# Splitting value tiles 1 to 3 of an attention projection into upper and lower parts, and reordering the last scores around state products (one Trainium2 core)

## The chip, the cores and the metric

One core of a Trainium2 chip (trn2) runs the whole program; the other cores are idle. The metric is the device time of one execution in microseconds. Three executions of the kernel before took 428.85 to 428.94 us, median 428.89 us. TensorE (PE in the profile), VectorE (DVE), ScalarE (ACT), GpSimd (POOL) and the DMA queues of SyncE (SP) each run their own instruction stream and meet at semaphores.

## The reference, cut to what matters

The program is one layer of a hybrid encoder on 512 tokens of width 1024, in float32. What the change touches is the attention group and, through queues and order, its two neighbours:

```python
z = x @ w_in                                  # x: 512 x 1024
u_pool, q, k, v, u_ssm = split(z)             # widths 256, 384, 384, 384, 384
y_pool = pool_mixer(u_pool, ...)              # trailing means over 2, 4, 8, 16 tokens, then a small product
s  = q k^T / 8 + bias, masked                 # 6 heads of 64, chunks of 64 tokens, 8 earlier chunks
y_attn = softmax(s) @ v
y_ssm = s5_mixer(u_ssm, ...)                  # state space, GELU, gated linear unit (GLU)
heads = concat(rms(y_pool), rms(y_attn), rms(y_ssm))
h = layer_norm(alpha * x + heads @ w_out)
# then a routed mixture of 16 experts, a gated per-layer embedding (PLE), and a second layer norm
```

## The kernel before, in words

Tokens are four tiles of 128. The input stands transposed in `xT` (region E, 8 blocks of 128 input channels by 512 tokens). A float32 product on TensorE is issued as two MATMUL records for each `matmul` call. The kernel already has a second way to make such a product: both operands are split into an upper part (ScalarE copies the tensor into a tile of type fp32r, which rounds it) and a lower part (VectorE subtracts the upper from the original, again as fp32r), and three fp32r products, upper by upper, lower by upper and upper by lower, are summed in PSUM with one MATMUL record each. The state input, queries, the first keys, the GLU (`glu`, L1139), the output projection and the PLE gate are made so.

Nothing is planned by a program: each engine's order is written out by hand, and semaphores join them. Around the change, from about 85 to 137 us of the span, the orders are these.

TensorE: `scores(1)`, value tile 0 (`v_tile`, L998, 8 calls of 128x384), the state products (L1117 to L1124: three groups of eight, two calls of 64 columns for each, into banks 7, 0, 6), `scores(2)` (L1126), value tile 1, the transposes of the softmax of heads 0 and 1 (`turn_probs`, L1040, three units of transposes for each head), value tile 2, heads 2 and 3, value tile 3, heads 4 and 5, then the GLU (L1171), the pooling product (L1179), `weigh_values` (L1061) and the output projection. `turn_probs` reuses three PSUM banks, so that each unit waits for the copy out of the unit three before it; heads 0, 1, 4, 5 are copied out by ScalarE (`pt_copy`), heads 2 and 3 by VectorE (`pt_move`, L1652).

VectorE: from `s_ready` (end of the state rotation) on it does `normalise` 0 and 1 (the softmax's division, L1581), `add_bias` 2 and 3 (scores out of PSUM, L1555), `row_max` 2 and 3 (L1573), `normalise` 2 and 3, the lower part of the GLU weights (L1644), `add_bias` 4 and 5, `row_max` 4 and 5, then three additions of the skip term to the state output (L1651, both tensors in SBUF), `normalise(4)`, `pt_move` 2 and 3, `normalise(5)` and the three lower parts of the GELU output (L1664).

ScalarE: copies of queries and keys out of PSUM, `pool_copy(1)`, the upper part of the GLU weights (L746), `v_copy(0)`, the exponents of heads 2 and 3 (`exps`, L723), three copies `y_copy` of the state output (L771), `v_copy(1)`, `pt_copy` 0 and 1, the exponents of heads 4 and 5, three GELUs (L789), their upper parts, `v_copy` 2 and 3, and so on.

The state output goes to DRAM and back in another layout on SyncE's queue: three transfers out, each after its `y_copy` (L370), and when all three have landed three back (L374), which L1651 waits for. Behind them on the same queue stand the loads of `w_out` (4096 KB), `x` (2048 KB) and the PLE gate weights.

GpSimd: after `pool_copy(1)` it makes the trailing means (`add_shift`, L559 to L574: L568 is the fourth step of ten) and signals `pool_ready`; later it adds squares (L580).

Of the kernel before, what the change touches and what calls it, by code (L numbers as in the profile page):

```python
# [19 lines left out]
ALU = mybir.AluOpType  # L20
ACT = mybir.ActivationFunctionType
AX = mybir.AxisListType

P = 128
D = 1024
T = 512
# [7 lines left out]
CH = 8  # L34
# [45 lines left out]
V_BANKS = (6, 7, 2, 5)  # L80
PM_BANKS = (7, 0)
# [32 lines left out]
def trunk(nc, io, out):  # L114
    with ExitStack() as ctx:
# [109 lines left out]
        def over(name, cols, at):  # L225
            return nc.alloc_sbuf_tensor_at(name, [P, cols], F32R, offset=at)
# [26 lines left out]

        pp_hi = over("ple_proj_upper", 2 * D, G0 + 4 * 2048)
# [7 lines left out]
        def dram(name, shape, dt=F32):  # L262
# [47 lines left out]
            "u_out u_back m0_in s_ready s_moved y_evac y_out y_back yin_ready gelu_done glu_lo_set glu_sig ssm_done "  # L310
# [19 lines left out]
        def _(sp):  # L330
            def load(dst, src, signal):
                sp.dma_start(dst, src).then_inc(S[signal], 16)
# [40 lines left out]
            for m in range(3):  # L373
                load(yT[:, m, :].rearrange("p (j c) -> p j c", j=CH), y_d.rearrange("j f c -> f j c")[m * P:(m + 1) * P], "y_back")  # L374

            sp.wait_ge(S["rot_ready"], 3)
            load(w_o, io["w_out"].rearrange("(k p) n -> p k n", p=P), "wo_in")

            sp.wait_ge(S["s_read"], HEADS)
            load(xh, io["x"].rearrange("(t p) d -> p t d", p=P), "xh_in")  # L380

            w_pg_v = io["w_ple_gate"].rearrange("(p k) n -> p k n", k=KD)
            load(w_pg[:, 0, 0:6], w_pg_v[:, 0:6, 0:512], "wpg0_in")
            sp.wait_ge(S["pool_ready"], 1)
# [97 lines left out]
        def _(gp):  # L482
# [84 lines left out]
            add_shift(b2, a, 2, 64, slice(0, 1))  # L567
            link(g.tensor_copy(a[64:P, 0:1], b2[64:P, 0:1]))  # L568
# [81 lines left out]
        def _(ac):  # L650
# [92 lines left out]
            qk_copy(5)  # L743
            pool_copy(1)
            ac.wait_ge(S["wglu_in"], 16)
# [34 lines left out]
            for m in range(3):  # L780
                y_copy(m)
# [3 lines left out]
            exps(4)  # L785
            exps(5)
# [35 lines left out]
            ac.wait_ge(S["wo_in"], 16)  # L822
# [123 lines left out]
        def _(pe):  # L946
# [55 lines left out]

            def scores(pair):
# [108 lines left out]
            v_tile(0, V_BANKS[0])  # L1112

# [11 lines left out]
            pe.wait_ge(S["s_read"], 4)  # L1125
            scores(2)  # L1126

            pe.wait_ge(S["y_evac"], 1)
            v_tile(1, V_BANKS[1])
            turn_probs(0)  # L1130
            turn_probs(1)
            v_tile(2, V_BANKS[2])
            turn_probs(2)
            turn_probs(3)
            v_tile(3, V_BANKS[3])
# [49 lines left out]
            pe.wait_ge(S["wo_in"], 16)  # L1185
# [254 lines left out]
        def _(dv):  # L1440
# [199 lines left out]
            row_max(3)  # L1640
            normalise(2)
# [3 lines left out]
            add_bias(4)  # L1645
            add_bias(5)
            row_max(4)
            row_max(5)
            dv.wait_ge(S["y_back"], 48)
# [8 lines left out]
            normalise(4)  # L1658
# [389 lines left out]
```

## Time and profile before

| | us |
|---|---|
| median of 3 executions | 428.89 |
| the profiled execution's own time | 429.05 |
| its span (first to last instruction) | 427.30 |
| TensorE busy in the span | 413.3 (97%) |
| VectorE busy | 255.4 (60%) |
| ScalarE busy | 129.6 (30%) |
| GpSimd busy | 93.6 (22%) |
| granted TensorE clock, mean | 0.993 of full |

Busy time counts every record; a MATMUL record lasts longer than the distance to the next one, since matmuls are pipelined. So for TensorE the distance between starts is what a product costs. In a timeline row the first number is the start in us from the span's start, the second the time to the end of the merged group, then engine, line, operation, output<-input, shapes, count, and in brackets the idle time before it and what ended it.

### The profile page before, as it was taken

The page shows a single profiled execution, that of the slowest core. Times are in us where ns is not written, and L with a number is a line of the kernel's source. Part 1 is how long each engine was busy: PE and PEld are TensorE (multiplying, and loading weights), DVE is VectorE, ACT ScalarE, POOL GpSimd, SP SyncE. Part 2 cuts the span into 40 slices and gives each one's busy share as a digit, 9 for nine tenths or more (in the row PEclk, how much of TensorE's full clock was granted, in tenths as well). Part 3 has the DMA queues.
Part 4 walks back from the last instruction along what each step waited for, and adds up shares of the span by engine and source line. Part 5 has one row for each costly group of instructions (what it writes and reads, how often), then busy time and mean ns, then how long its engine had stood idle before and what let it go on. Part 6 is the DMA issues. An engine that isn't in the chain of part 4 may idle for free.

```text
span 427.3 us, 5594 instructions
## 1 busy us (share of the span) xinstructions
PE 413.3 (97%) x2167; PEld 238.1 (56%) x2167; DVE 255.4 (60%) x464; ACT 129.6 (30%) x235; POOL 93.6 (22%) x132
## 2 busy tenths in 40 slices
PE   8899999999999999999999999999999999999992
PEld 5677655469667555676577887333333433333271
DVE  2999985986873999998867524211101112224987
ACT  4721336025497890200621011011110111111243
POOL 2830269275000800000000742010111111000000
PEclk9999999999999999999999999999999999999997
DMA  7994103251997891111490428999999999977313
GB/s 264 431 397 129 49 2 66 68 130 51 276 411 295 285 392 63 49 49 51 158 384 8 191 43 325 425 410 413 418 417 418 421 411 411 423 289 247 152 45 153
DMA packets 33626, 102.76 MB, mean 240 GB/s; under 512 B 14882, under 2 KB 16082, under 8 KB 26816
## 3 DMA queue, kind: packets, MB, share of 16 engines
q1 hardware_dynamic: 26032, 92.79, 56.1%
q0 software_dynamic: 4016, 7.97, 5.6%
q10 hardware_dynamic: 3552, 1.65, 1.4%
q8 instruction: 17, 0.28, 0.3%
q14 instruction: 9, 0.07, 0.1%
HBM read 93.29 MB, written 15.24 MB: 254 GB/s over the span
## 4 chain that ended last, share of the span: by engine, by line
PE 67%; issue 23%; DVE 4%; DMA 3%; POOL 1%; ACT 1%; DVEq 0%; POOLq 0%; ACTq 0%
PE bank L1307 20%; PE bank L1317 10%; PE bank L952 7%; PE bank L1000 5%; PE bank L1302 3%; PE bank L967 3%; PE bank L992 3%; PE bank L1009 2%; PE bank L988 2%; PE bank L1067 2%; PE bank L1057 2%; POOL slot_scratch L595 1%; PE bank L995 1%; PE bank L1123 1%; PE bank L1122 1%
## 5 line engine op out<-in xcount | busy, mean ns | idle before, releaser
L1307 PE MATMUL bank<-region_a,region_g 128*64 128x512 f32 (+1 forms) x224 | 77.8, 594 | 0.0
L1317 PE MATMUL bank<-region_a,region_c 128*64 128x512 f32 (+1 forms) x160 | 43.7, 596 | 0.0
L1885 DVE TENSOR_TENSOR region_c<-region_c,bank 128x256 f32<-128x256 f32 x12 | 5.1, 421 | 64.6 <-ACT region_c L907 64.6
L1307 PE MATMUL bank<-region_h,region_g 128*64 128x512 f32 (+1 forms) x96 | 42.4, 594 | 0.0
L1307 PE MATMUL bank<-region_b,region_g 128*64 128x512 f32 (+1 forms) x96 | 42.4, 594 | 0.0
L1307 PE MATMUL bank<-region_c,region_g 128*32 128x512 f32 (+1 forms) x96 | 42.4, 594 | 0.0
L1878 DVE COPY region_g<-bank 128x512 f32<-128x512 f32 x24 | 15.5, 687 | 40.4 <-PE bank L1302 40.4
L1307 PEld LDWEIGHTS bank<-region_a,region_g 128*64 128x64 f32 (+1 forms) x224 | 22.2, 123 | 25.1 <-issue 24.4
L1151 PE MATMUL bank<-region_b,region_e 128*128 128x512 f32 x68 | 32.9, 607 | 0.0
L907 ACT ACTIVATE region_c<-bank 128x256 f32<-128x256 f32 x12 | 4.6, 384 | 83.9 <-PE bank L1307 83.9
L952 PE MATMUL bank<-region_e,region_a 128*128 128x512 f32 x64 | 28.0, 595 | 0.0
L595 POOL DMA_INDIRECT slot_scratch<-region_h,slot_i x8 | 8.2, 1027 | 88.3 <-issue 88.3
L1235 PE MATMUL bank<-ple_gate_upper,hidden_upper 128*128 128x512 f32 x64 | 25.7, 402 | 0.0
L1237 PE MATMUL bank<-ple_gate_upper,hidden_lower 128*128 128x512 f32 x64 | 25.0, 390 | 0.0
L1236 PE MATMUL bank<-ple_gate_lower,hidden_upper 128*128 128x512 f32 x64 | 24.9, 390 | 0.0
L1317 PEld LDWEIGHTS bank<-region_a,region_c 128*64 128x64 f32 (+1 forms) x160 | 12.0, 123 | 22.1 <-issue 22.0
L1317 PE MATMUL bank<-region_c 128*32 128x512 f32 (+1 forms) x48 | 21.9, 596 | 0.0
L1317 PE MATMUL bank<-region_b,region_c 128*64 128x512 f32 (+1 forms) x48 | 21.7, 595 | 0.0
L1000 PE MATMUL bank<-region_a,region_e 128*128 128x384 f32 x64 | 21.5, 489 | 0.0
L952 PEld LDWEIGHTS bank<-region_e,region_a 128*128 128x128 f32 x64 | 12.0, 190 | 14.5 <-issue 14.4
L608 POOL DMA_INDIRECT expert_scratch<-region_g,region_h x5 | 5.0, 1002 | 65.2 <-ACT region_g L890 65.2
L1722 DVE SCALAR_TENSOR_TENSOR region_f<-bank,rms_r,region_f 128x512 f32<-128x512 f32 x24 | 18.0, 750 | 2.0 <-PE bank L1151 1.3
(364 smaller groups left out, 881.9 us busy)
## 6 DMA issues: line engine op xcount, KB each, us to landing
region_a<-in_w_exp_down SPq DMA_DIRECT2D x10, 1024.0 KB, 14.4
region_a<-in_w_exp_gate SPq DMA_DIRECT2D x7, 1024.0 KB, 8.4
region_a<-in_w_exp_up SPq DMA_DIRECT2D x7, 1024.0 KB, 12.1
region_b<-in_w_out SPq DMA_DIRECT2D x1, 4096.0 KB, 14.7
expert_scratch<-zero_scratch SPq DMA_DIRECT2D x8, 512.0 KB, 9.5
region_c<-in_w_ple_gate SPq DMA_DIRECT2D x2, 1536.0 KB, 23.1
region_b<-in_w_exp_gate SPq DMA_DIRECT2D x3, 1024.0 KB, 10.3
region_b<-in_w_exp_up SPq DMA_DIRECT2D x3, 1024.0 KB, 12.3
```

The lines of the kernel that those rows point to most:

```text
L952: last = mm(bank[bank_i][:], w[:, k, m * P:(m + 1) * P], xT[:, k, :], start=(k == 0), stop=(k == KD - 1))
L967: last = mm(bank[m][:], w[:, k * SSM_W + m * P:k * SSM_W + (m + 1) * P], x[:, k * T:(k + 1) * T], start=False, stop=(stop and k == 5))
L992: mm(dst, w_hi[:, k * width + m * P:k * width + (m + 1) * P], x[:, k * T:(k + 1) * T], start=False, stop=False)
L1000: last = mm(bank[bank_i][:, 0:ATT_W], xT[:, k, t * P:(t + 1) * P], w_v[:, k, :], start=(k == 0), stop=(k == KD - 1))
L1151: last = mm(bank[WO_AT[half][group]][:], hdT[:, k, t * P:(t + 1) * P], w_o[:, k, half * 512:half * 512 + 512], start=(i == 0), stop=(i == ...
L1235: mm(bank[PG_AT[k % 2]][:], h_hi[t][:, x], pg_hi[:, w], start=(c == 0), stop=False)
L1236: mm(bank[PG_AT[k % 2]][:], h_hi[t][:, x], pg_lo[:, w], start=False, stop=False)
L1237: last = mm(bank[PG_AT[k % 2]][:], h_lo[t][:, x], pg_hi[:, w], start=False, stop=(c == KD - 1))
L1307: return mm(out_[at:at + width].rearrange("p (u n) -> p u n", u=2), x[:, k, at:at + width], w[:, k], start=(k == 0), stop=(k == KD - 1), t ...
L1317: return mm(bank[banks[half]][at:at + width, :], act_e[:, r, 2, k * P + at:k * P + at + width], w[:, k, half * 512:half * 512 + 512], star ...
L1722: last = stt(xh[:, t, cols], bank[WO_AT[half_][group]][:], rms_r[:, group, t:t + 1], xh[:, t, cols], ALU.mult, ALU.add)
L1878: v.tensor_copy(hgT[:, t % 2, 4 * u:4 * u + 4, :], bank[B_TOK[u]][:].rearrange("p (k s) -> p k s", k=4)).then_inc(S["hgT_evac"], 1)
```

## The change

Value tiles 1 to 3 are made by a new function `v_split`: 24 fp32r products in place of 8 float32 calls. The upper parts of the value weights and of `xT` are made by ScalarE in two pieces each, between the copies it does from 80 us on. The lower part of the input is made by GpSimd in the middle of the pooling, in place over `xT`, after value tile 0 has read it; GpSimd then waits until five heads are normalised before it goes on with the pooling. The lower part of the value weights is made by VectorE. `scores(2)` goes ahead of the state products. On VectorE `add_bias` and `row_max` of heads 4 and 5 and `normalise(4)` move ahead; on ScalarE the exponents of heads 4 and 5 go between the three `y_copy`. The last quarter of `w_out`, the first half of the PLE gate weights and `x` are loaded only after value tile 3, since the new tiles lie where they land.

The list of semaphores (`y_back` goes, `gp_lo_set` comes) is left out of the diff.

```diff
@@ -78,6 +78,7 @@
 KERN_BANKS = (1, 2)
 X_BANKS = ((3, 7), (0, 6))
 V_BANKS = (6, 7, 2, 5)
+XV_PARTS, WV_PARTS = ((0, 5), (5, KD)), ((0, 6), (6, KD))
 PM_BANKS = (7, 0)
 Y_BANKS = (7, 0, 6)
 PV_BANKS = (5, 6, 3)
@@ -251,6 +252,13 @@
         kw_lo = over("key_weights_lower", 6 * ATT_W, A0 + 4 * (O_K + 2 * ATT_W))
         uw_lo = over("state_weights_lower", 6 * SSM_W, A0 + 4 * 2 * SSM_W)
 
+        F0 = R0 + 4 * 4096
+        XV_AT, WV_AT = (F0 + 4 * 1536, B0 + 4 * 6656), (C0 + 4 * 768, A0 + 4 * 13440)
+        xv_hi = [over(f"value_input_upper{i}", (hi - lo) * T, XV_AT[i]) for i, (lo, hi) in enumerate(XV_PARTS)]
+        wv_hi = [over(f"value_weights_upper{i}", (hi - lo) * ATT_W, WV_AT[i]) for i, (lo, hi) in enumerate(WV_PARTS)]
+        xv_lo = over("value_input_lower", KD * T, R0)
+        wv_lo = over("value_weights_lower", KD * ATT_W, A0 + 4 * O_V)
+
         pp_hi = over("ple_proj_upper", 2 * D, G0 + 4 * 2048)
         pp_lo = over("ple_proj_lower", 2 * D, H0)
         p_hi = over("ple_input_upper", 2 * T, G0 + 4 * 1024)
@@ -371,16 +379,18 @@
                              y_ch[:, 8 * m:8 * m + 8, :].rearrange("p g c -> p (g c)")).then_inc(S["y_out"], 16)
             sp.wait_ge(S["y_out"], 48)
             for m in range(3):
-                load(yT[:, m, :].rearrange("p (j c) -> p j c", j=CH), y_d.rearrange("j f c -> f j c")[m * P:(m + 1) * P], "y_back")
+                load(yT[:, m, :].rearrange("p (j c) -> p j c", j=CH), y_d.rearrange("j f c -> f j c")[m * P:(m + 1) * P], "y_out")
 
             sp.wait_ge(S["rot_ready"], 3)
-            load(w_o, io["w_out"].rearrange("(k p) n -> p k n", p=P), "wo_in")
-
+            w_o_v = io["w_out"].rearrange("(k p) n -> p k n", p=P)
+            load(w_o[:, 0:6], w_o_v[:, 0:6], "wo_in")
+            sp.wait_ge(S["pe_v"], NT)
+            load(w_o[:, 6:KD], w_o_v[:, 6:KD], "wo_in")
+
+            w_pg_v = io["w_ple_gate"].rearrange("(p k) n -> p k n", k=KD)
+            load(w_pg[:, 0, 0:6], w_pg_v[:, 0:6, 0:512], "wpg0_in")
             sp.wait_ge(S["s_read"], HEADS)
             load(xh, io["x"].rearrange("(t p) d -> p t d", p=P), "xh_in")
-
-            w_pg_v = io["w_ple_gate"].rearrange("(p k) n -> p k n", k=KD)
-            load(w_pg[:, 0, 0:6], w_pg_v[:, 0:6, 0:512], "wpg0_in")
             sp.wait_ge(S["pool_ready"], 1)
             load(w_pg[:, 1, 2:8], w_pg_v[:, 2:8, 512:D], "wpg_in")
             sp.wait_ge(S["pe_pm"], 2)
@@ -565,6 +575,13 @@
             add_shift(a, plT, 1, 0, both)
             add_shift(b2, a, 2, 0, second)
             add_shift(b2, a, 2, 64, slice(0, 1))
+            gp.wait_ge(S["xw_hi_set"], 12)
+            gp.wait_ge(S["pe_v"], 1)
+            for (lo, hi), upper in zip(XV_PARTS, xv_hi):
+                at = slice(lo * T, hi * T)
+                g.tensor_tensor(xv_lo[:, at], RE[:, at], upper[:], ALU.subtract).then_inc(S["gp_lo_set"], 1)
+            gp.wait_ge(S["gp_lo_set"], 2)
+            gp.wait_ge(S["p_norm"], HEADS - 1)
             link(g.tensor_copy(a[64:P, 0:1], b2[64:P, 0:1]))
             add_shift(a, b2, 4, 0, second)
             link(g.tensor_copy(b2[64:P, 1:2], a[64:P, 1:2]))
@@ -741,7 +758,18 @@
             exps(1)
             qk_copy(4)
             qk_copy(5)
+
+            def value_weights_upper(i):
+                at = slice(O_V + WV_PARTS[i][0] * ATT_W, O_V + WV_PARTS[i][1] * ATT_W)
+                a.activation(wv_hi[i][:], RA[:, at], ACT.Copy).then_inc(S["xw_hi_set"], 1)
+
+            ac.wait_ge(S["wv_in"], 32)
+            value_weights_upper(0)
             pool_copy(1)
+            value_weights_upper(1)
+            ac.wait_ge(S["s_ready"], 1)
+            for (lo, hi), upper in zip(XV_PARTS, xv_hi):
+                a.activation(upper[:], RE[:, lo * T:hi * T], ACT.Copy).then_inc(S["xw_hi_set"], 1)
             ac.wait_ge(S["wglu_in"], 16)
             a.activation(wg_hi[:], w_glu.rearrange("p k n -> p (k n)"), ACT.Copy).then_inc(S["gelu_done"], 1)
 
@@ -777,13 +805,14 @@
             exps(2)
             exps(3)
             ac.wait_ge(S["s_moved"], 64)
-            for m in range(3):
-                y_copy(m)
+            y_copy(0)
+            exps(4)
+            y_copy(1)
+            exps(5)
+            y_copy(2)
             v_copy(1)
             pt_copy(0)
             pt_copy(1)
-            exps(4)
-            exps(5)
             for m in range(3):
                 ac.wait_ge(S["yin_ready"], m + 1)
                 a.activation(geluT[:, m, :].rearrange("p (c j) -> p c j", j=CH),
@@ -819,7 +848,7 @@
             ac.wait_ge(S["pool_mixed"], 2)
             for k in WO_SPLIT:
                 a.activation(hd_hi[k][:], hdT[:, k, P:T], ACT.Copy).then_inc(S["wo_hi_set"], 1)
-            ac.wait_ge(S["wo_in"], 16)
+            ac.wait_ge(S["wo_in"], 32)
             for k in (0, 1, 5, 6, 7):
                 a.activation(wo_hi[k][:], w_o[:, k, :], ACT.Copy).then_inc(S["wo_hi_set"], 1)
 
@@ -1000,6 +1029,21 @@
                     last = mm(bank[bank_i][:, 0:ATT_W], xT[:, k, t * P:(t + 1) * P], w_v[:, k, :], start=(k == 0), stop=(k == KD - 1))
                 last.then_inc(S["pe_v"], 1)
 
+            def v_split(t, bank_i):
+
+                def upper(parts, homes, width, k, at, w):
+                    i = 0 if k < parts[0][1] else 1
+                    first = (k - parts[i][0]) * width + at
+                    return homes[i][:, first:first + w]
+
+                for term, (signal, count) in enumerate((("xw_hi_set", 12), ("gp_lo_set", 2), ("xw_lo_set", 10))):
+                    pe.wait_ge(S[signal], count)
+                    for k in range(KD):
+                        x = xv_lo[:, k * T + t * P:k * T + t * P + P] if term == 1 else upper(XV_PARTS, xv_hi, T, k, t * P, P)
+                        w = wv_lo[:, k * ATT_W:(k + 1) * ATT_W] if term == 2 else upper(WV_PARTS, wv_hi, ATT_W, k, 0, ATT_W)
+                        last = mm(bank[bank_i][:, 0:ATT_W], x, w, start=(term == 0 and k == 0), stop=(term == 2 and k == KD - 1))
+                last.then_inc(S["pe_v"], 1)
+
             def scores(pair):
 
                 def part(odd, tile):
@@ -1110,6 +1154,8 @@
             scores(1)
             pe.wait_ge(S["wv_in"], 32)
             v_tile(0, V_BANKS[0])
+            pe.wait_ge(S["s_read"], 4)
+            scores(2)
 
             pe.wait_ge(S["s_moved"], 64)
             pe.wait_ge(S["m0_in"], 16 * CH * 2)
@@ -1122,17 +1168,15 @@
                     mm(dst, m0[:, g].rearrange("p l h -> p (l h)"), uch[:, g, :], start=True, stop=False)
                     last = mm(dst, cp[:, g, 1:CH + 1, :].rearrange("p l h -> p (l h)"), s_in[:, g, :], start=False, stop=True)
                 last.then_inc(S["pe_y"], 1)
-            pe.wait_ge(S["s_read"], 4)
-            scores(2)
 
             pe.wait_ge(S["y_evac"], 1)
-            v_tile(1, V_BANKS[1])
+            v_split(1, V_BANKS[1])
             turn_probs(0)
             turn_probs(1)
-            v_tile(2, V_BANKS[2])
+            v_split(2, V_BANKS[2])
             turn_probs(2)
             turn_probs(3)
-            v_tile(3, V_BANKS[3])
+            v_split(3, V_BANKS[3])
             turn_probs(4)
             turn_probs(5)
 
@@ -1182,7 +1226,7 @@
             for pair in range(3):
                 weigh_values(pair)
 
-            pe.wait_ge(S["wo_in"], 16)
+            pe.wait_ge(S["wo_in"], 32)
             pe.wait_ge(S["pool_mixed"], 2)
             pe.wait_ge(S["glu_sig"], 3)
             pe.wait_ge(S["sq_added"], 3)
@@ -1638,15 +1682,21 @@
             add_bias(3)
             row_max(2)
             row_max(3)
+            add_bias(4)
+            add_bias(5)
+            row_max(4)
+            row_max(5)
+            dv.wait_ge(S["xw_hi_set"], 10)
+            dv.wait_ge(S["pe_v"], 1)
+            for (lo, hi), upper in zip(WV_PARTS, wv_hi):
+                tt(wv_lo[:, lo * ATT_W:hi * ATT_W], RA[:, O_V + lo * ATT_W:O_V + hi * ATT_W], upper[:],
+                   ALU.subtract).then_inc(S["xw_lo_set"], 1)
             normalise(2)
             normalise(3)
             dv.wait_ge(S["gelu_done"], 1)
             tt(wg_lo[:], w_glu.rearrange("p k n -> p (k n)"), wg_hi[:], ALU.subtract).then_inc(S["glu_lo_set"], 1)
-            add_bias(4)
-            add_bias(5)
-            row_max(4)
-            row_max(5)
-            dv.wait_ge(S["y_back"], 48)
+            normalise(4)
+            dv.wait_ge(S["y_out"], 96)
             for m in range(3):
                 stt(yT[:, m, :], uT[:, m, :], vec[:, V_D + m:V_D + m + 1], yT[:, m, :], ALU.mult, ALU.add).then_inc(S["yin_ready"], 1)
             def pt_move(h):
@@ -1655,7 +1705,6 @@
                     dv.wait_ge(S["pe_pt"], k + 1)
                     v.tensor_copy(probT[h // 2][:, h % 2, o:o + w], bank[PT_BANKS[k % 3]][:, 0:w]).then_inc(S["pt_moved"], 1)
 
-            normalise(4)
             pt_move(2)
             pt_move(3)
             normalise(5)
```

## Rows read from the trace of the kernel before

**Rows 1.** The page's chain that ended last: share of the span by engine

```profile
PE 67%; issue 23%; DVE 4%; DMA 3%; POOL 1%; ACT 1%; DVEq 0%; POOLq 0%; ACTq 0%
```

**Rows 2.** Timeline of PE, 78 to 95 us: start, us, engine, line, operation, shapes, count

```profile
94.44 0.33 PE L1122 MATMUL bank<-region_h 128*128 128x64 f32 x2
```

**Rows 3.** Timeline of PE, 95 to 160 us, same columns

```profile
105.20 2.43 PE L1009 MATMUL bank<-region_g 64*128 64x256 f32 x16
107.56 5.43 PE L1000 MATMUL bank<-region_a,region_e 128*128 128x384 f32 x16
...
115.32 5.33 PE L1000 MATMUL bank<-region_a,region_e 128*128 128x384 f32 x16
120.48 1.25 PE L1057 MATMUL bank<-ident,region_a 128*128 128x128 f32 x10
121.96 1.38 PE L1057 MATMUL bank<-ident,region_a 128*128 128x128 f32 x10 [0.22 <-DVE region_a L1656]
...
131.07 0.39 PE L1144 MATMUL bank<-gelu_lower,glu_upper 128*128 128x512 f32 x1
...
136.76 0.40 PE L1145 MATMUL bank<-gelu_upper,glu_lower 128*128 128x512 f32 x1
```

**Rows 4.** Timeline of VectorE (DVE), 66 to 162 us: scores, row maxima, softmax, moves

```profile
89.29 0.62 DVE L1569 SCALAR_TENSOR_TENSOR region_a<-bank,region_f 128x128 f32<-128x128 f32 x2 [1.29 <-PE bank L1009]
...
92.98 3.23 DVE L1578 TENSOR_REDUCE att_mx<-region_a 128x1 f32<-128x128 f32 x8
...
98.05 4.58 DVE L1587 TENSOR_SCALAR region_a<-region_a,att_sm 128x128 f32<-128x128 f32 x4
...
102.75 1.27 DVE L1587 TENSOR_SCALAR region_a<-region_a,att_sm 128x128 f32<-128x128 f32 x4
103.94 1.35 DVE L1644 TENSOR_TENSOR glu_lower<-region_a,glu_upper 128x1152 fp32r<-128x1152 f32 x1
...
114.51 2.07 DVE L1651 SCALAR_TENSOR_TENSOR region_h<-region_h,vec 128x512 f32<-128x512 f32 x3
...
121.12 3.15 DVE L1656 COPY region_a<-bank 128x512 f32<-128x512 f32 x6 [0.78 <-PE bank L1057]
```

**Rows 5.** Timeline of ScalarE (ACT), 66 to 162 us

```profile
93.66 1.17 ACT L746 ACTIVATE glu_upper<-region_a 128x1152 fp32r<-128x1152 f32 x1 [6.13 <-DMA region_a<-in_w_glu]
...
95.10 0.39 ACT L729 ACTIVATE region_a<-region_a,att_mx 128x128 f32<-128x128 f32 x1
...
100.32 0.58 ACT L773 ACTIVATE region_b<-bank 128x512 f32<-128x512 f32 x1
...
105.31 0.60 ACT L773 ACTIVATE region_b<-bank 128x512 f32<-128x512 f32 x1 [2.98 <-PE bank L1123]
```

**Rows 6.** Timeline of GpSimd (POOL), 66 to 162 us: the pooling

```profile
92.80 0.61 POOL L568 COPY region_c<-region_c 64x512 f32<-64x512 f32 x1
...
95.77 1.25 POOL L562 TENSOR_TENSOR region_c<-region_c 64x504 f32<-64x504 f32 x1
97.10 2.36 POOL L573 TENSOR_TENSOR region_c<-region_c 128x1024 f32<-128x1024 f32 x1
99.53 2.48 POOL L574 TENSOR_TENSOR region_c<-region_c,region_g 128x1024 f32<-128x1024 f32 x1
```

**Rows 7.** Tile y_scratch, 108.95 to 109.3 us: the last transfer back, issue and landing

```profile
L332 SPq DMA_DIRECT2D region_h<-y_scratch x1: 880/880/880, 109.0 to 109.0; - x1
...
DMA to landing us min/median/max: 4.6/4.6/4.6
```

**Rows 8.** Timeline of GpSimd (POOL), 66 to 162 us: later sums

```profile
140.26 3.72 POOL L580 TENSOR_TENSOR region_g<-region_g,region_a 128x512 f32<-128x512 f32 x2 [0.51 <-ACT region_a L769]
```

**Rows 9.** Timeline of VectorE (DVE), 66 to 162 us: later differences

```profile
140.67 2.18 DVE L1672 TENSOR_TENSOR ple_gate_lower<-region_c,ple_gate_upper 128x1024 fp32r<-128x1024 f32 x1
...
144.57 1.22 DVE L1672 TENSOR_TENSOR ple_gate_lower<-region_c,ple_gate_upper 128x1024 fp32r<-128x1024 f32 x1
```

**Rows 10.** The page's DMA issues: KB each, us from issue to landing

```profile
region_b<-in_w_out SPq DMA_DIRECT2D x1, 4096.0 KB, 14.7
```

More of the change, by code:

```diff
@@ L309, in trunk @@
             "kern_in kern_done rot_ready xrot_done "
-            "u_out u_back m0_in s_ready s_moved y_evac y_out y_back yin_ready gelu_done glu_lo_set glu_sig ssm_done "
+            "u_out u_back m0_in s_ready s_moved y_evac y_out gp_lo_set yin_ready gelu_done glu_lo_set glu_sig ssm_done "
             "pool_ready pool_mixed pe_u pe_qk pe_pool pe_v pe_bxT pe_kern pe_x pe_s pe_pt pe_pv pe_pm pe_y "
```

## The prediction, made before the change was run

> **What bounds the kernel now.** I read the page's busy shares and its chain first: TensorE is busy 97% of the span and holds most of the chain [rows 1] (the part called issue begins behind 149 us and runs past a stretch in which TensorE's records stand back to back, so I take it as TensorE time too). Then I read TensorE's timeline through the changed stretch. From the first state product at 94.44 us [rows 2] to the GLU near 131 us it has one idle gap of 0.22 us, before the transposes of head 3 at 121.96 us, which waited for VectorE's copy L1656 [rows 3]. So a product made shorter here is worth its full length, as long as every new helper is early enough, and anything that makes VectorE late at L1656 is paid in full. That gap is the place to watch: value tiles 1 and 2 lie ahead of it, only tile 3 behind it.
>
> **The value tiles.** Value tile 2 starts at 115.32 us and the next transposes at 120.48 us: 5.16 us for 16 records of 384 columns, 0.322 us each [rows 3]. The price of an fp32r product is in the GLU: from its record at 131.07 us to that at 136.76 us are 25 starts, 5.69 us, 0.228 us for 512 columns [rows 3]. No row has 384 columns of fp32r. From below: all of it scales with the columns, 0.171 us. From above: it doesn't shrink at all, 0.228 us. A moving tile is read column by column in either type, so I take a value near the lower end, with a little of the 0.228 us fixed: 0.174 us. 24 of them are 4.18 us, 0.98 us less for each tile (bounds: 1.06 less, 0.31 more). Three tiles: 2.9 us less if nothing waits.
> On this the Trainium skill (TensorE: Matmul & The Clock Gate, Back-to-back issue gap) gives columns over 2.4 GHz plus 2.5 ns, an estimate of 162 ns for 384 columns; the GLU's rows are 12 ns above that formula. By it each tile would gain 1.3 us.
>
> **scores(2) ahead of the products.** The two only change places: the scores take 2.36 us (105.20 to 107.56), the products 10.76 us [rows 2, 3]. The scores wait for `add_bias(3)`, which ended with the start of the row maxima at 92.98 us [rows 4], before 94.44 us: no wait. The products now run from 96.8 to 107.56 us, and value tile 1 starts at 107.56 us, as before. Their three groups end 2.4 us later each.
>
> **The helpers of the split.** ScalarE copies 7168 columns more, at 1.17 us for 1152 about 7.3 us; it stood idle 6.1 us before 93.66 us and about as long between the earlier key and pool copies [rows 5], so it is done by about 92.5 us: nothing. If that cover were gone, 7.3 us would fall on `exps`.
> GpSimd waits for value tile 0 (94.7 us). 1024 columns of a two-tensor operation take 2.36 us [rows 6]; 4096 columns 9.1 to 9.4 us, so it is done at 104.0 us. TensorE wants this part at 107.56 + 1.4 = 109.0 us: nothing. VectorE's operations in that time are scores from PSUM and row maxima. Eight row maxima took 3.23 us, 0.4 us each, with GpSimd busy beside them from 92.80 us on [rows 4, 6]: no room for a wait on a sum of 1 us or more, so these don't disturb each other. Scores of two heads took 3.69 us (89.29 to 92.98 us).
> VectorE: `add_bias` 4 and 5 from 96.9 to 100.6, `row_max` to 103.8 us. The lower weights, 2304 and 768 columns at 1.35 us for 1152 [rows 4], are 3.5 us; they begin when GpSimd's second piece ends, 104.1 us, and end at 107.5 us, wanted at 110.3 us: nothing. Then `normalise` 2 and 3 (1.4 us each with the reciprocal), the GLU's lower weights 1.3 us, `normalise(4)`: 113.0 us. Here GpSimd goes on.
>
> **The two engines meet.** The rest of the pooling ran from 92.80 to 102.01 us; its third sum starts 2.97 us after L568 and lasts 1.25 us, then come two of 1024 columns [rows 6]. Begun at 113.1 us, that third sum runs from 116.0 to 117.3 us and the rest to 122.3 us.
> The state output: `y_copy(0)` at 100.5 us, exponents of head 4 from 102.3 us (its row maxima end there) for 2.61 us (two heads from 95.10 to 100.32 us [rows 5]), `y_copy(1)`, exponents of head 5 to 108.1 us, `y_copy(2)` to 108.7 us instead of 105.9 us. The last transfer back was issued at 109.0 us and landed 4.6 us later, 113.6 us [rows 7]; now 116.4 us.
> At 116.4 us VectorE wants L1651, three operations on two SBUF tensors (2.07 us together [rows 4]), while GpSimd is in that third sum. What happens then is in two places. L1587, 1.27 us when alone, took 4.58 us from 98.05 us, until both large pooling sums were over [rows 4, 6]. And L1672 (two SBUF tensors) took 2.18 us beside GpSimd's L580 and 1.22 us where it came first, while the two L580 took 3.72 us, not 2 times 1.27 us or less [rows 8, 9]: the engines take turns, each operation waits for the other engine's present one. So: first L1651 at 117.3 us, 0.66 us; a large sum, 2.28 us; second L1651; the second large sum; third L1651, ending at 117.3 + 3 x 0.66 + 2 x 2.25 = 123.8 us. Bounds: 118.5 us with no turns at all, 123.8 us with all; I take the upper, since L1651 is nearest to L1672 in its operands.
> The Trainium skill (SBUF — State Buffer, the section on two separate sides) says why: VectorE and GpSimd share one port pair under an exclusive lock, and a VectorE operation with two SBUF inputs takes it too. The trace agrees for L1672; for a SCALAR_TENSOR_TENSOR like L1651 no row shows it.
>
> **What is late next.** Behind L1651 on VectorE stand the copies L1656 of head 2. They began at 121.12 us before; TensorE would now be ready for them at 119.2 us, but gets them from 123.8 us: 2.7 us later than before, all that tiles 1 and 2 gained lost. Head 3's transposes start 2.7 us late, tile 3 gives 1.0 us back, and the GLU starts 1.7 us late. Its lower GELU parts (the last L1651 123.8, a GELU, upper copies, `normalise(5)`, L1664) are ready near 130.3 us, the GLU wants them at 132.4 us: hidden. From there all is TensorE again and shifts as a whole.
>
> **The queues.** On SyncE's queue 3072 KB of w_out leave as before; 1024 KB, then 1536 KB of PLE gate weights and `x` now wait for tile 3 (about 130 us). 4096 KB landed in 14.7 us [rows 10], so the first 2560 KB need at most 9.2 us, 139.5 us, about when VectorE is through with the GLU's gates; `x` is wanted 20 us later. I cost it at nothing; without that cover 1 us on VectorE. `pool_ready`, 22 us later than before, holds back a PLE load that already waits in the queue, and a TensorE wait that comes after the GLU: nothing.
>
> **The sum.** 429.05 + 2.7 - 1.0 = 430.75 us against the profiled execution; that stood 0.16 us above the median, so 430.6 us.
>
> **The rivals.** A measurement of this kernel can tell about 0.2% (0.86 us) from no change.
> (a) VectorE's L1651 takes no turns with GpSimd. It ends at 118.5 us, L1656 follows TensorE, and all three tiles count: 428.9 - 2.9 = 426.0 us, faster. For it: the row maxima were not held up, and L1651 is another kind of operation than L1672. Against: it reads two tensors in SBUF, as L1672 does. It decides from the point at which L1651 ends before 119.2 us. Chance 0.27.
> (b) They take turns, but the transfer lands before the third sum begins, or VectorE reaches 113.0 us half a microsecond later. Only 0.4 us lie between 116.0 and 116.4 us. Then the first L1651 goes ahead of that sum and one turn of 2.3 us falls away: L1651 ends at 121.5 us, 0.4 us of delay against 1.0 us gained, 428.3 us. Chance 0.2.
> (c) fp32r with 384 columns costs as with 512: tile 3 is 0.3 us longer instead of 1.0 us shorter, 431.9 us with the turns. Against: float32 records do shrink with their columns. Chance 0.03.
> (d) The change doesn't do what it says: the tiles wait for their lower parts. VectorE is 2.8 us early, GpSimd 5 us; it would take an operation nearly half as slow again. Included in 0.02 for anything else, such as a late load.
>
> **How the numbers follow.** My case has chance 0.48; with (c) and half of the rest slower has 0.52. (b) is within 0.2%: 0.19. Faster is (a) and a little of (b): 0.29. The likeliest case's own range is 429.9 to 431.2 us (a turn's start 0.7 us either way); for 8 in 10 it reaches down to (a), 425.8 us, and up to 431.4 us.
>
> **What would show it.** Right: L1651 takes about 7 us for three in place of 2.07; TensorE waits 4 to 5 us for L1656 before head 3; tiles 1 to 3 last 4.2 us each. The GLU starts near 132.5 us. Wrong: three L1651 in about 2.1 us beside busy GpSimd; no TensorE wait for L1656; a GLU at 127.8 us; or a wait at the second or third term of value tile 1.

## The result, and the profile after

The changed kernel took 432.37 us (median of five executions: 431.33, 431.35, 432.37, 432.45, 432.46) against 428.89 us for the kernel before: 3.5 us slower between the medians; the ratio over all executions, two of which were 1 us faster than the other three, is 1.0069 with a 95% interval of 1.0058 to 1.0080. The forecast was 430.6 us, range 425.8 to 431.4: the right side, half the size, and the range missed by 1 us. The profiled execution has 432.37 us and a span of 430.6 us, 3.3 us more than the 427.3 us of before. Its TensorE is busy 96% of the span and its mean granted clock over the span is 0.987 of full, 0.993 before. The other two executions near 432.4 us show 0.987 too, the two at 431.3 us 0.990 and 0.991.

TensorE's timeline through the changed stretch (start, us, then as before; L1044 is `v_split`, L1101 `turn_probs`, L1188 the GLU):

```profile
107.51 1.66 PE L1044 MATMUL bank<-value_weights_upper,value_input_upper 128*128 128x384 f32 x8
109.01 1.55 PE L1044 MATMUL bank<-value_weights_upper,value_input_lower 128*128 128x384 f32 x8
110.40 1.55 PE L1044 MATMUL bank<-value_weights_lower,value_input_upper 128*128 128x384 f32 x8
...
118.45 1.25 PE L1101 MATMUL bank<-ident,region_a 128*128 128x128 f32 x10
123.80 2.37 PE L1101 MATMUL bank<-ident,region_a 128*128 128x128 f32 x10 [4.10 <-DVE region_a L1706]
125.82 2.91 PE L1044 MATMUL bank<-value_weights_upper,value_input_upper 128*128 128x384 f32 x8
128.53 1.92 PE L1044 MATMUL bank<-value_weights_upper,value_input_lower 128*128 128x384 f32 x8
130.28 1.55 PE L1044 MATMUL bank<-value_weights_lower,value_input_upper 128*128 128x384 f32 x8
131.67 2.66 PE L1101 MATMUL bank<-ident,region_a 128*128 128x128 f32 x20
...
134.40 0.40 PE L1188 MATMUL bank<-gelu_lower,glu_upper 128*128 128x512 f32 x1
```

Value tile 1 starts at 107.51 us, where before it started at 107.56 [rows 3]. Eight fp32r products of 384 columns take 1.39 us (109.01 to 110.40), 0.174 us each, and tile 1 lasts to 111.78 us, 4.3 us in place of 5.2. Then the transposes of head 3 wait 4.10 us for VectorE's copy. And behind this wait everything on TensorE is slow: the transposes of head 3 take from 123.80 to 125.82 us, 2.02 us where ten others cost some 1.2, and tile 3's three groups of eight take 2.7, 1.75 and 1.39 us. The GLU's second product comes at 134.40 us instead of 131.07 [rows 3]: 3.33 us, the whole difference of the spans.

Busy time of each engine in stretches behind the wait (the first number behind the last engine, POOL, is the granted TensorE clock):

```profile
core 0: us, PE busy (x) PEld busy (x) DVE busy (x) ACT busy (x) POOL busy (x), PEclk, DMA share, GB/s
118.00:124.00 6.00, 1.90 (x15) 1.66 (x14) 6.00 (x4) 2.70 (x3) 4.43 (x2) 0.87 0.89 358
124.00:126.00 2.00, 2.00 (x11) 2.00 (x11) 1.50 (x4) 1.97 (x5) 0.00 (x0) 0.50 0.06 23
126.00:128.00 2.00, 2.00 (x8) 2.00 (x8) 1.97 (x7) 0.25 (x1) 0.00 (x0) 0.50 0.00 0
128.00:130.00 2.00, 2.00 (x10) 2.00 (x9) 2.00 (x4) 0.00 (x0) 0.00 (x0) 0.67 0.00 0
130.00:132.00 2.00, 2.00 (x15) 1.97 (x13) 0.01 (x1) 0.13 (x1) 0.00 (x0) 1.00 0.00 0
```

The granted clock is 0.50, the lower level of 1.2 GHz, from 122.5 us, when TensorE had stood idle since 119.7 us, to past 129 us, and full again from 129.5 us on. The Trainium skill (TensorE: Matmul & The Clock Gate, part on the clock gate) says that TensorE drops to half its clock after idling and comes back only after work. The trace agrees, with 0.50 in these rows. It is a price that the prediction didn't have.

VectorE's and GpSimd's timelines (L1692 the lower value weights, L1631 `normalise`, L1701 the skip additions, L1706 the copies of heads 2 and 3; L582 the lower input, L572 and L590, L591 sums of the pooling):

```profile
103.71 3.42 DVE L1692 TENSOR_TENSOR value_weights_lower<-region_a,value_weights_upper 128x2304 fp32r<-128x2304 f32 x2
...
111.32 1.27 DVE L1631 TENSOR_SCALAR region_a<-region_a,att_sm 128x128 f32<-128x128 f32 x4
116.11 6.94 DVE L1701 SCALAR_TENSOR_TENSOR region_h<-region_h,vec 128x512 f32<-128x512 f32 x3 [3.51 <-DMA region_h<-y_scratch]
122.97 1.61 DVE L1706 COPY region_a<-bank 128x512 f32<-128x512 f32 x3
```

```profile
94.65 9.05 POOL L582 TENSOR_TENSOR value_input_lower<-region_e,value_input_upper 128x2560 fp32r<-128x2560 f32 x2 [2.18 <-PE bank L1029]
112.73 0.61 POOL L585 COPY region_c<-region_c 64x512 f32<-64x512 f32 x1 [9.03 <-DVE region_a L1631]
...
115.70 1.26 POOL L572 TENSOR_TENSOR region_c<-region_c 64x504 f32<-64x504 f32 x1
117.05 2.70 POOL L590 TENSOR_TENSOR region_c<-region_c 128x1024 f32<-128x1024 f32 x1
119.83 2.68 POOL L591 TENSOR_TENSOR region_c<-region_c,region_g 128x1024 f32<-128x1024 f32 x1
```

The three skip additions took 6.94 us, not 2.07 [rows 4]. They came at 116.11 us, while the third sum of the pooling ran (115.70 to 116.96 us); each of the two large sums, 2.37 us when nothing of VectorE's takes turns with it (e8), shows 2.7 us here, since each began by waiting for the end of an addition. The engines took turns, as L1672 and L580 did before [rows 8, 9].

### The profile page after: what moved, and what is told of

The parts are those of the page before. It is cut to its first block, busy times and chain, and to the rows that moved or that the text cites. A ratio compares the mean times of both kernels' runs of the same rounds, so it can differ in the third digit from the quotient of the medians.

```text
span 430.6 us, 5655 instructions
## 1 busy us (share of the span) xinstructions
PE 413.5 (96%) x2191; PEld 244.4 (57%) x2191; DVE 260.4 (60%) x466; ACT 136.0 (32%) x239; POOL 102.5 (24%) x134
## 4 chain that ended last, share of the span: by engine, by line
PE 61%; issue 23%; DVE 7%; DMA 4%; ACT 3%; POOL 1%; SPq 0%; DVEq 0%; POOLq 0%; ACTq 0%
PE bank L1351 20%; PE bank L1361 10%; PE bank L981 6%; PE bank L1346 3%; PE bank L996 3%; PE bank L1021 3%; PE bank L1053 2%; DVE region_h L1701 2%; PE bank L1017 2%; PE bank L1111 2%; POOL slot_scratch L612 1%; PE bank L1044 1%; PE bank L1024 1%; PE bank L1029 1%; ACT region_a L746 1%
## 5 line engine op out<-in xcount | busy, mean ns | idle before, releaser
L1351 PEld LDWEIGHTS bank<-region_h,region_g 128*64 128x64 f32 (+1 forms) x96 | 11.4, 123 | 12.5 <-issue 12.2
```

Of the source, the lines that this page charges most:

```text
L1351: return mm(out_[at:at + width].rearrange("p (u n) -> p u n", u=2), x[:, k, at:at + width], w[:, k], start=(k == 0), stop=(k == KD - 1), t ...
```

## The experiments

All are made from the changed kernel, each timed in five rounds beside the kernel before on the same chip (its medians there are 428.96 to 429.10 us; the changed kernel's time is that of the result above). The two questions: is it GpSimd's turns that make VectorE late and so cost TensorE its wait, and is the rest of the loss the clock?

### e1: the pooling goes on only after the skip additions

```diff
             gp.wait_ge(S["p_norm"], HEADS - 1)
+            gp.wait_ge(S["yin_ready"], 3)
```

> GpSimd goes on with the pooling only when VectorE's three skip additions (L1651 of before) are done. Theory (the two engines take turns, and the delay of the copies of head 2 is what TensorE pays): the three additions take 2.1 us in place of 6.9, TensorE doesn't wait before head 3, its granted clock stays at full, and the three tiles take 4.2 us each. But the pooling now meets normalise(5) and the lower GELU parts on VectorE, which end near 130 us, so TensorE waits about 2 us before the GLU: 428.3 us. Rival (the additions are slow for another reason, such as the w_out transfer beside them): still 6.9 us, time 432.4 us. Rival (fp32r products of these operands are slow by themselves): tile 3 still 5.8 us and the time at least 429.5 us.

Measured: 428.25 us (427.81 to 430.27), ratio 0.9992 (0.9981 to 1.0004). VectorE's rows, and what TensorE waited for:

```profile
115.88 2.08 DVE L1702 SCALAR_TENSOR_TENSOR region_h<-region_h,vec 128x512 f32<-128x512 f32 x3 [3.38 <-DMA region_h<-y_scratch]
118.97 3.14 DVE L1707 COPY region_a<-bank 128x512 f32<-128x512 f32 x6 [1.02 <-PE bank L1102]
...
122.24 5.64 DVE L1632 TENSOR_SCALAR region_a<-region_a,att_sm 128x128 f32<-128x128 f32 x4
```

```profile
PE bank L1102 <- DVE region_a L1632: 1.5, 1, 1.5
...
PE bank L1188 <- DVE gelu_lower L1714: 0.5, 1, 0.5
```

The additions take 2.08 us, with the same w_out transfer beside them, so it was GpSimd. TensorE waits 0.22 us before head 3, as in the kernel before. But the pooling now takes its turns with `normalise(5)`, 5.64 us in place of 1.28, and TensorE waits 1.5 us before head 5 and 0.5 us before the GLU: some 2 us, as expected, but most of it two steps earlier. The wait was moved some 7 us down the line. It wasn't harmless there in every execution: eight of the twelve took 427.8 to 428.5 us with a mean clock of 0.993 to 0.996, the profiled one among them (1.00 behind the wait), and four took 429.5 to 430.3 us with 0.990 to 0.991. These four fit a fall of the clock that no profile shows.

### e2: TensorE kept busy during the wait

```diff
             turn_probs(2)
+            for _ in range(19):
+                mm(bank[4][:], xv_lo[:, 0:P], xv_lo[:, 0:T], start=True, stop=True)
             turn_probs(3)
```

> As after, but TensorE makes 19 fp32r products of 512 columns into an unused bank between the transposes of heads 2 and 3, 4.3 us in place of the 4.1 us wait; nothing reads them. Theory (tile 3 was slow since the granted clock fell to 1.2 GHz after the idle 4.1 us): the granted clock stays at full, tile 3 takes 4.2 us in place of 5.8, time about 430.6 us, which is what was forecast. Rival (tile 3 is slow because of its operands or of transfers beside it): tile 3 still 5.8 us, time 432.5 us or more.

Measured: 430.14 us (429.96 to 430.64), ratio 1.0027 (1.0016 to 1.0038). TensorE's timeline and two stretches:

```profile
119.51 4.61 PE L1179 MATMUL bank<-value_input_lower 128*128 128x512 f32 x19
123.95 1.33 PE L1101 MATMUL bank<-ident,region_a 128*128 128x128 f32 x10
125.04 1.64 PE L1044 MATMUL bank<-value_weights_upper,value_input_upper 128*128 128x384 f32 x8
...
129.29 2.66 PE L1101 MATMUL bank<-ident,region_a 128*128 128x128 f32 x20
```

```profile
120.00:130.00 10.00, 10.00 (x59) 9.01 (x59) 9.38 (x16) 4.85 (x8) 2.61 (x1) 1.00 0.31 123
130.00:140.00 10.00, 9.88 (x48) 7.29 (x48) 3.44 (x6) 7.66 (x14) 0.55 (x1) 1.00 0.91 352
```

TensorE reaches head 3 at 123.95 us, 0.15 us later than in the changed kernel, and yet the program is 2.2 us faster. The clock is 1.00 throughout, tile 3 takes 4.25 us (125.04 to 129.29) in place of 5.85, head 3 takes 1.1 us in place of 2.0. Operands, transfers and order are those of the changed kernel; only the idle stretch is gone. So the fall of the clock cost 2.2 us in the median execution, and what is left, 1.1 us over the kernel before, is the lateness of head 3 (2.0 us) less tile 3's gain. Also the two groups of the changed kernel's times, 431.3 and 432.4 us, are one group here (429.96 to 430.64 us, mean clock 0.993 to 0.995). With the mean clocks of the two groups, 0.990 to 0.991 and 0.987, this fits a lower clock that lasted for different times from execution to execution; no profile of the faster group shows it.

### e7: half of the wait busy

```diff
             turn_probs(2)
+            for _ in range(9):
+                mm(bank[4][:], xv_lo[:, 0:P], xv_lo[:, 0:T], start=True, stop=True)
             turn_probs(3)
```

> As e2, but 9 products, 2.05 us, so that some 2 us of TensorE's wait for VectorE stay idle. Theory (it is the length of the idle stretch that brought the clock down; the 1.8 us wait of e3 left it at full): full clock, tile 3 in 4.2 us, 430.2 us as e2. Rival (a wait there brings the clock down whatever its length): tile 3 longer than 4.5 us and 431.3 us or more.

Measured: 430.26 us (430.16 to 430.48 in four executions, 431.72 in the fifth), ratio 1.004 (1.0027 to 1.0053). What TensorE waited for, and its clock:

```profile
PE bank L1101 <- DVE region_a L1708: 2.1, 1, 2.1
```

```profile
120.00:130.00 10.00, 7.91 (x50) 7.12 (x49) 9.40 (x16) 4.74 (x8) 2.63 (x1) 1.00 0.32 131
```

Idle for 2.1 us, TensorE keeps its clock (1.00), and the time is e2's. The fifth execution, 1.5 us slower, isn't the profiled one, but its mean clock over the span is 0.991, against 0.993 to 0.994 in the other four: most likely the clock fell in it. So the length of the wait counts (four executions of five come out as the theory has it, while at 4.1 us the mean clock is lower in all five), but it doesn't decide alone: 2.1 us cost only themselves as a rule, and once some 1.5 us more.

### e3: GpSimd isn't held at all

```diff
-            gp.wait_ge(S["p_norm"], HEADS - 1)
```

> GpSimd doesn't wait for the fifth normalised head: the pooling goes on at 103.8 us. Theory (turns): it now takes turns with the lower value weights and normalise 2 to 4 on VectorE; each of them waits for a pooling operation, normalise(4) ends near 120 us instead of 112.7, the skip additions then run undisturbed but late, to about 123 us, and the time stays within 1 us of 432.4 us. Rival (only the skip additions suffer): the pooling is over before 116 us, the additions take 2.1 us, 426.0 us.

Measured: 427.69 us (427.56 to 427.89), ratio 0.9967 (0.9954 to 0.9980): between the two expectations, nearer to the rival's, and faster than the kernel before. VectorE, GpSimd, and TensorE's wait:

```profile
103.88 3.41 DVE L1691 TENSOR_TENSOR value_weights_lower<-region_a,value_weights_upper 128x2304 fp32r<-128x2304 f32 x2
...
112.10 3.52 DVE L1696 TENSOR_TENSOR glu_lower<-region_a,glu_upper 128x1152 fp32r<-128x1152 f32 x1
...
118.87 2.07 DVE L1700 SCALAR_TENSOR_TENSOR region_h<-region_h,vec 128x512 f32<-128x512 f32 x3
```

```profile
103.92 3.85 POOL L584 COPY region_c<-region_c 64x512 f32<-64x512 f32 x1
...
114.48 3.40 POOL L590 TENSOR_TENSOR region_c<-region_c,region_g 128x1024 f32<-128x1024 f32 x1
```

```profile
PE bank L1100 <- DVE region_a L1705: 1.8, 1, 1.8
```

VectorE and GpSimd did meet, but the turns were not strict: GpSimd's copy at 103.92 us, 0.61 us when alone, waited through both parts of the lower value weights (3.85 us), `normalise(4)` ended at 118.9 us, not 120, and the skip additions followed at once. They ran undisturbed in 2.07 us. TensorE waited 1.8 us at full clock, and all five executions lie within 0.3 us. With the large sums where the change has them, the hold for `normalise` is therefore what hurts: it shields operations that nobody waits for and puts the pooling's largest sums beside the three that TensorE is waiting for.

### e8: the copies ahead of the skip additions

```diff
             normalise(4)
-            dv.wait_ge(S["y_out"], 96)
-            for m in range(3):
-                stt(yT[:, m, :], ...)
...
             pt_move(2)
             pt_move(3)
+            dv.wait_ge(S["y_out"], 96)
+            for m in range(3):
+                stt(yT[:, m, :], ...)
             normalise(5)
```

> As after, hold and all, but VectorE makes the copies of heads 2 and 3 ahead of the three skip additions. Theory (what cost the time is that these copies stood behind additions which waited for GpSimd's turns): no TensorE wait over 0.3 us before head 3, full clock; the additions come at about 122 us, when the pooling is over, and take 2.1 us; the lower GELU parts come at about 128.7 us against a GLU that could start at 127.8: 427.0 us. Rival (the additions' lateness itself costs what it did, through the GELU): 430 us or more.

Measured: 430.12 us median of 12 executions, in two groups (428.3 to 428.9 and 430.0 to 430.4), ratio 1.0016 (1.0005 to 1.0027). A miss in the time, which is the rival's (430 us or more). TensorE's waits and its clock:

```profile
PE bank L1101 <- ACT region_a L784: 2.7, 1, 2.7
...
PE bank L1101 <- DVE region_a L1703: 0.2, 1, 0.2
```

```profile
120.00:130.00 10.00, 7.34 (x50) 6.98 (x51) 7.46 (x16) 6.97 (x12) 1.85 (x1) 0.98 0.68 243
130.00:140.00 10.00, 10.00 (x39) 7.41 (x39) 3.30 (x6) 6.26 (x10) 0.42 (x1) 0.85 1.03 400
```

The part about head 3 held: 0.2 us. But the additions came at 122.1 us and the GELUs behind them, and on ScalarE's queue the copies `pt_copy(4)` stand behind the GELUs: TensorE waited 2.7 us for ScalarE before head 5, which I had not followed. It is the way of the rival, lateness through the GELU, with another wait at its end. In the profiled execution the clock fell again (0.85 in the next 10 us). The two groups of times fit executions with and without that fall: the eight slower ones have a mean clock of 0.989 to 0.991, the profiled one among them, the four faster ones 0.993 to 0.994.

### e5 and e6: each half of the change alone

e5 keeps the new order and makes tiles 1 to 3 as in the kernel before; e6 keeps the tiles in parts and puts `scores(2)`, heads 4 and 5 and `normalise(4)` where they were. Neither holds GpSimd.

```diff
-            v_split(1, V_BANKS[1])
+            v_tile(1, V_BANKS[1])
...
-            add_bias(4)
-            add_bias(5)
-            row_max(4)
-            row_max(5)
             dv.wait_ge(S["xw_hi_set"], 10)
```

(the first two lines are e5's, for each tile, with the upper and lower parts taken out; the rest is e6's, which puts the four lines behind the GLU's lower weights again and the exponents behind `pt_copy(1)`)

> The order of after (scores(2) ahead of the state products, heads 4 and 5 ahead on VectorE and ScalarE, the later loads), but value tiles 1 to 3 as float32 products and no upper or lower parts; the pooling isn't held and runs in one piece as before. Theory (the order alone only changes places): the skip additions come at 116 us instead of 114.5, take 2.1 us and are over before the copies of head 2 at 121.1 us, time 428.9 us, no change. Rival (the later round trip of the state output costs by itself): TensorE waits 1 us or more before the GLU, 430 us or more.

Measured: 429.21 us (428.89 to 429.51), ratio 1.0006 (0.9998 to 1.0015): no difference. TensorE's only wait in the stretch is the old one of 0.2 us.

> The other half alone: tiles 1 to 3 in parts, but scores(2), the exponents, the row maxima of heads 4 and 5 and normalise(4) in the order of before; the pooling isn't held. Theory (the gain of the tiles is 2.9 us and only a late VectorE takes it away): GpSimd's lower input part ends about 104 us, the pooling then runs to about 116 us and delays the skip additions by 1 to 2 turns, to about 118 us; the exponents of heads 4 and 5 stand before the GELU as before, so the lower GELU parts come about 128.4 us where the GLU could start at 127.8: 426.7 us. Rival (the reordering is needed, since the lower parts are late without it): a TensorE wait at value tile 1 and 428.5 us or more.

Measured: 434.49 us (434.20 to 434.87), ratio 1.013 (1.0116 to 1.0145). VectorE, TensorE's wait, and a stretch with the granted clock:

```profile
96.75 9.96 DVE L1686 TENSOR_TENSOR value_weights_lower<-region_a,value_weights_upper 128x2304 fp32r<-128x2304 f32 x2
...
111.51 3.51 DVE L1691 TENSOR_TENSOR glu_lower<-region_a,glu_upper 128x1152 fp32r<-128x1152 f32 x1
114.94 0.61 DVE L1611 SCALAR_TENSOR_TENSOR region_a<-bank,region_f 128x128 f32<-128x128 f32 x2
```

```profile
PE bank L1100 <- DVE region_a L1611: 6.1, 1, 6.1
```

```profile
118.00:124.00 6.00, 5.24 (x21) 5.24 (x22) 5.83 (x13) 3.69 (x11) 0.00 (x0) 0.50 0.41 162
```

A clear miss. The lower value weights, 3.4 us of work, are asked for at 96.75 us beside GpSimd's lower input, and take 9.96 us in turns; after them `normalise` and the GLU's lower weights take turns with the pooling, and `add_bias` of heads 4 and 5 comes at 114.94 us instead of 107.67 in the kernel before. TensorE needs their banks for the first transposes and waits 6.1 us, and behind this wait its clock is 0.50 too (118 to 124 us). The sum fits: 6.1 us less the 2.9 us of the tiles is 3.2 us, and the other 2.3 us of the 5.5 us lost is about what the clock cost in the changed kernel. Against e3, which has the parts, no hold and the new order, the old order costs 6.8 us. So the reordering is needed for the parts: it fills the time of GpSimd's lower input with work on PSUM and row maxima, which show no turns (eight row maxima take 3.2 us beside GpSimd's lower input, as before). In itself it neither costs nor gives (e5).

### e4, e9, e10: the two large sums wait for the lower GELU parts

```diff
             gp.wait_ge(S["rc_in"], 16)
+            gp.wait_ge(S["glu_lo_set"], 4)
             link(g.tensor_tensor(a, a, rcnt, ALU.mult))
```

> GpSimd makes the small pooling steps as in after, but its two sums of 1024 columns wait until VectorE has made the lower GELU parts. Theory: only the third pooling step stands before the skip additions, which end near 119 us instead of 123; no TensorE wait before head 3 to speak of, full clock, GLU near 127.8 us, the pooling ready near 130.5 us before TensorE wants it at 134 us: 426.0 us, the full gain of the three tiles. Rival (something else on VectorE or the lower GELU parts binds, and the tiles' gain isn't to be had): 428.5 us or more.

Measured: 426.12 us (425.70 to 426.27), ratio 0.9929 (0.9916 to 0.9942). VectorE and GpSimd:

```profile
116.26 2.60 DVE L1702 SCALAR_TENSOR_TENSOR region_h<-region_h,vec 128x512 f32<-128x512 f32 x3 [3.65 <-DMA region_h<-y_scratch]
119.13 3.15 DVE L1707 COPY region_a<-bank 128x512 f32<-128x512 f32 x6 [0.27 <-PE bank L1102]
...
123.59 1.89 DVE L1714 TENSOR_TENSOR gelu_lower<-region_h,gelu_upper 128x512 fp32r<-128x512 f32 x3
```

```profile
115.72 1.27 POOL L572 TENSOR_TENSOR region_c<-region_c 64x504 f32<-64x504 f32 x1
125.65 2.36 POOL L591 TENSOR_TENSOR region_c<-region_c 128x1024 f32<-128x1024 f32 x1 [8.66 <-DVE gelu_lower L1714]
128.09 2.41 POOL L592 TENSOR_TENSOR region_c<-region_c,region_g 128x1024 f32<-128x1024 f32 x1
```

One turn is left (2.60 us for the three additions), TensorE waits the old 0.2 us, its clock stays full, and the pooling is done at 130.5 us, before TensorE asks for it at 134.03 us. The GLU's second product comes at 128.09 us, 3.0 us earlier than in the kernel before. The tiles in parts are worth what their rows say.

> As e4 (the two sums of 1024 columns wait for the lower GELU parts), and the wait for the fifth normalised head is taken away, so that the small pooling steps start at 103.8 us beside the lower value weights. Theory: the small steps take a few turns on VectorE before 112 us, where it is some 3 us ahead of its next work, and none is left beside the skip additions, which take 2.1 us in place of 2.6; TensorE doesn't need them earlier: 426.1 us, the same as e4. Rival (the hold is worth something, since it keeps the lower weights or normalise(2) in time): a TensorE wait at value tile 1 or head 2 and 427 us or more.

Measured: 426.28 us (426.12 to 426.36), ratio 0.9931 (0.9917 to 0.9944): the same. The additions take 2.08 us, and `normalise(4)` ends 2 us later, where nobody waits.

> The same kernel as e4 once more, beside e9 on the same chip: 426.1 us, 0.7% under the kernel before. If e4's gain was luck of one chip, it is closer to 429.

Measured: 426.33 us (425.79 to 426.54), ratio 0.9929 (0.9915 to 0.9942). e4 holds: 2.8 us under the kernel before on the same chip, and 6 us under the changed one, with one line more than the latter.

## Why the prediction was right in kind and wrong in size

**The value tiles: right.** 0.174 us for a product of 384 columns was the value taken, 0.174 us is what 109.01 to 110.40 us gives; e4 shows the 2.9 us of three tiles as time. The Trainium skill's formula (TensorE: Matmul & The Clock Gate, Back-to-back issue gap), by which the prediction gave an estimate of 162 ns, is 12 ns low here, as it was for the GLU's rows.

**Order and helpers: right.** Tile 1 started within 0.1 us of the forecast and waited for none of its parts: GpSimd's was done at 103.7 us (104.0 forecast), VectorE's at 107.1 (107.5), `normalise(4)` at 112.6 (113.0). e5 shows the order costs nothing. That transfers behind tile 3 cost nothing is borne out by e4, where they too leave only after tile 3 and the whole 2.9 us arrives.

**The turns: right, slightly too dear.** The round trip of the state output landed at 116.1 us (116.4 forecast), inside the third sum, so rival (b) with its margin of 0.4 us didn't come about. The additions ended at 123.05 us, not 123.8. Rival (a), no turns, falls with e1: the same additions, 6.94 us with GpSimd beside them and 2.08 us without. A SCALAR_TENSOR_TENSOR with two SBUF tensors takes turns as the TENSOR_TENSOR of [rows 9] does, and the Trainium skill's rule on the shared port pair (SBUF — State Buffer, the section on two separate sides) holds for it.

**What is late next: right, and 0.85 us too dear.** The copies of head 2 started 1.85 us later than before (2.7 forecast), and TensorE waited 4.1 us (4 to 5 forecast).

**The step that failed** is the sum's last part: tile 3 gives 1.0 us back, and "from there all is TensorE again and shifts as a whole". It priced all work behind the wait at full clock. Between the start of head 3's transposes and the GLU's second product lie 10.60 us (123.80 to 134.40); before it was 9.11 us (121.96 to 131.07 [rows 3]), and by the forecast 8.1. The missing 2.5 us are head 3's transposes (0.8 us over) and tile 3 (1.67 us over), at a granted clock of 0.50. With it the sum is 1.84 - 1.0 + 2.5 = 3.3 us, the difference of the spans. Two errors of opposite sign stand in the forecast: the lateness of head 3 was put 0.85 us too high, which hid a third of the 2.5 us. e2 takes the idle stretch away and leaves all else: 430.14 us, 0.5 us from the forecast of 430.6. No row of the kernel before shows this fall in mid-kernel, since its longest wait in that stretch is 0.22 us. But its trace shows it at the end, where TensorE has been idle since 419 us:

```profile
423.00:425.00 2.00, 0.00 (x0) 0.00 (x0) 1.79 (x4) 0.00 (x0) 0.00 (x0) 0.50 0.57 231
```

A forecast of a 4 us wait on TensorE should have asked for its price. The range's upper end, which took only (c) and a turn's start into account, was too low for that reason.

**Rival (c)** (a product of 384 columns at the price of 512) is out by the same rows. **(d)** is out: no tile waited for its parts, in e6 neither (tile 1 ran from 107.33 to 111.61 us). What e6 shows is another danger of the same kind: without the reordering VectorE is 7 us late with the scores of heads 4 and 5.

What stays open: when the clock falls and how long it stays down. The length of the wait alone doesn't tell it: by the mean clocks and the times it seems to have fallen in four of twelve executions of e1 (waits of 1.5 and 0.5 us), in none of five of e3 (1.8 us), in one of five of e7 (2.1 us), in eight of twelve of e8 (2.7 us) and in all five of the changed kernel (4.1 us). Only one execution of each kernel has a profile.

## What to carry to other kernels

When a step is given to GpSimd or put beside it, list VectorE's operations with two SBUF tensors (and its scalings in SBUF) that would meet it, and look which of them heads the queue for TensorE: a wait that holds GpSimd away from one of them pushes it onto the next, so hold it until the last one that TensorE waits for, as e4's one line does. When a forecast puts an idle stretch of some microseconds into a TensorE that was never idle, let the range hold a price for the clock beside the wait: 4.1 us of waiting cost 6.3 us here in the median execution, and waits of 1.5 to 2.7 us cost some 1.5 us more than themselves in some executions and nothing more in others.

## What was not expected of the hardware

- The turns of VectorE and GpSimd are not strictly one and one. In e3 a GpSimd copy waited 3.2 us through two VectorE subtractions issued back to back (3.85 us against 0.61), where in the changed kernel a sum got its turn after each addition.
- The clock: idle stretches of 1.5 us (e1), 1.8 us (e3) and 2.1 us (e7) left the granted clock at 1.00 in the profiled executions; behind 2.7 us (e8) it fell (0.85 over 10 us); behind 4.1 us (the changed kernel) and 6.1 us (e6) it was 0.50. The same kernel doesn't behave alike each time: e1, e7 and e8 have slower executions with lower mean clocks (0.989 to 0.991) beside faster ones (0.993 to 0.996), some 1.5 us apart.
